# 16-bit split operands for the scores and index logits of the two A mixers

## What is computed

```python
q  = _rope(q.reshape(B, T, N_HEADS, HEAD_DIM), pos)      # 8 heads of 64
k  = _rope(k.reshape(B, T, N_HEADS, HEAD_DIM), pos)
qi = _rope(qi.reshape(B, T, IDX_HEADS, IDX_DIM), pos)    # 8 index heads of 64
ki = _rope(ki[:, :, None, :], pos)[:, :, 0, :]           # one index key
logits = jnp.einsum('bqhd,bsd->bqhs', qib, k_idx)
score = jnp.einsum('bqhs,bqh->bqs', jax.nn.relu(logits), wb) * idx_scale
score = jnp.where(causal[None], score, -jnp.inf)
_, sel = lax.top_k(score, topk)                          # 64 keys of each query
s = jnp.einsum('bqhd,bqkhd->bhqk', qb, k_sel) * att_scale
p = jax.nn.softmax(jnp.where(valid[:, None], s, -jnp.inf), axis=-1)
out = jnp.einsum('bhqk,bqkhd->bqhd', p, v_sel)
```

## Time and profile before

| | us |
|---|---|
| median of 3 runs | 1520.39 (1520.13 to 1520.46) |
| the profiled execution, its own time | 1520.18 |
| its span in the trace | 1518.1 |
| PE busy | 1510.1 (99%) |
| DVE busy | 637.6 (42%) |
| ACT busy | 475.0 (31%) |
| POOL busy | 1027.0 (68%) |
| mean granted clock of PE | 0.999 of full |

### The profile page before, as it was taken

How to read it: one execution, slowest core, us unless ns; L and a number is a source line. 1 busy time by engine, 2 the same in 40 slices (tenths; PEclk the granted TensorE clock), 3 DMA queues, 4 the chain that set the end, 5 groups by cost and what they waited for, 6 DMA issues and landing times.

```text
span 1518.1 us, 32667 instructions
## 1 busy us (share of the span) xinstructions
PE 1510.1 (99%) x13880; PEld 1174.1 (77%) x13882; DVE 637.6 (42%) x1509; ACT 475.0 (31%) x1243; POOL 1027.0 (68%) x565
## 2 busy tenths in 40 slices
PE   9999999999999999999999999999999999999998
PEld 7666888898666866669889966669888889888885
DVE  4332385445332333315844533325454535464532
ACT  3221163413221132204541232213443313343322
POOL 6976667667767677775586677773858565648653
PEclk9999999999999999999999999999999999999999
DMA  9665554455655565555545465664455554546551
GB/s 390 224 212 200 183 189 173 167 179 217 210 200 198 192 237 207 194 202 196 175 167 186 176 236 194 204 211 156 161 198 193 183 195 155 177 150 239 170 192 56
DMA packets 42625, 293.96 MB, mean 194 GB/s; under 512 B 4720, under 2 KB 5232, under 8 KB 8688
## 3 DMA queue, kind: packets, MB, share of 16 engines
q1 hardware_dynamic: 41760, 290.83, 54.5%
q10 hardware_dynamic: 720, 1.04, 0.2%
HBM read 290.81 MB, written 1.05 MB: 192 GB/s over the span
## 4 chain that ended last, share of the span: by engine, by line
PE 97%; DVE 2%; ACT 1%; issue 0%; DVEq 0%
PE ps L774 26%; PE ps L656 15%; PE ps L657 15%; PE ps L658 15%; PE ps L775 13%; PE ps L675 1%; PE ps L677 1%; PE ps L676 1%; PE ps L869 1%; PE ps L889 1%; ACT ps L1308 1%; PE ps L823 0%; PE ps L734 0%; PE ps L824 0%; PE ps L825 0%; PE ps L851 0%
## 5 line engine op out<-in xcount | busy, mean ns | idle before, releaser
L626 POOL TENSOR_TENSOR w_low<-ring 128x1024 f16<-128x1024 f32 (+1 forms) x544 | 1008.2, 1880 | 379.0 <-DMA ring<-in_w 378.7
L656 PE MATMUL ps<-hP,ring 128*128 128x256 f16 (+1 forms) x1936 | 469.1, 257 | 0.8 <-DVE work L1957 0.4
L657 PE MATMUL ps<-hP,ring 128*128 128x256 f16 (+1 forms) x1936 | 468.9, 257 | 0.0
L658 PE MATMUL ps<-hP,w_low 128*128 128x256 f16 (+1 forms) x1936 | 468.8, 257 | 0.0
L774 PE MATMUL ps<-hP,ring 128*128 128x512 f16 x1280 | 416.3, 380 | 0.0
L775 PE MATMUL ps<-hP,w_low 128*128 128x256 f16 x1280 | 349.2, 273 | 0.0
L774 PEld LDWEIGHTS ps<-hP,ring 128*128 128x128 bf16 x1280 | 125.0, 98 | 151.5 <-issue 0.4
L656 PEld LDWEIGHTS ps<-hP,ring 128*128 128x128 bf16 x1936 | 189.9, 98 | 23.3 <-issue 5.4
L657 PEld LDWEIGHTS ps<-hP,ring 128*128 128x128 bf16 x1936 | 189.2, 98 | 15.6
L658 PEld LDWEIGHTS ps<-hP,w_low 128*128 128x128 f16 x1936 | 189.2, 98 | 15.5
L774 PE MATMUL ps<-work,ring 128*128 128x512 f16 x528 | 171.8, 380 | 0.0
(11 more groups left out here) (277 smaller groups left out, 1740.8 us busy)
## 6 DMA issues: line engine op xcount, KB each, us to landing
ring<-in_w SPq DMA_DIRECT2D x261, 1024.0 KB, 4.8
ring<-in_w SPq DMA_DIRECT2D x12, 512.0 KB, 3.6
con<-in_const SPq DMA_DIRECT2D x1, 2812.0 KB, 18.3
gm<-in_gm SPq DMA_DIRECT2D x2, 1024.0 KB, 17.8
ring<-in_w SPq DMA_DIRECT2D x2, 768.0 KB, 4.9
ring<-in_w SPq DMA_DIRECT2D x2, 560.0 KB, 5.4
ring<-in_w SPq DMA_DIRECT2D x2, 544.0 KB, 3.5
xT<-in_x SPq DMA_DIRECT2D x3, 256.0 KB, 4.1
```

Of the source, the lines that this page charges most:

```text
L626: nc.gpsimd.tensor_tensor(w_low[:, c % SLOTS, a:b], ring[:, c % SLOTS, a:b], w_high[:, c % SLOTS, a:b], ALU.subtract).then_inc(split.by((c ...
L656: nc.tensor.matmul(bank, w_high[:, slot, a:a + m], rhs(k, 0), start=(k == 0), stop=False)
L657: nc.tensor.matmul(bank, w_high[:, slot, a:a + m], rhs(k, 1), start=False, stop=False)
L658: mm = nc.tensor.matmul(bank, w_low[:, slot, a:a + m], rhs(k, 0), start=False, stop=(k == kt - 1))
```

## The change

The rotated q, k, qi and ki are kept as fp16 high and low parts in `rotP`, which lies where `rot` lay. DVE's `rope` writes its sum back to the tile's PSUM bank and signals `roped_in`. ACT's new `high` copies it to the high part (`rot_high`), and DVE's new `low` subtracts and signals `taken_dve`. There are 13 such tiles in a mixer. Logits and scores take three 16-bit passes, with two heads alternating; `scores_16` (line 855) was there before for the B mixers. In PE's order one more q tile stands ahead of the first logits, and one more tile ahead of `turn(0)` and of what follows it. The rest keeps its order. The diff, cut to its core:

```diff
+IN_PARTS_A = ('q', 'k', 'qi', 'ki')
+        rotP, _ = pairs(e, 13)
         rot, e = area(e, 13, T)
 ... PE
                     def logits(p):
                         for h in (2 * p, 2 * p + 1):
-                            b = 4 + h % 3
                             if h == 0:
                                 pe.wait_ge(*taken(s, ("ki", 0)))
                             elif h < 3:
                                 pe.wait_ge(*taken(s, ("wi", h - 1)))
                             else:
                                 pe.wait_ge(*relu_done.at((s, h - 3)))
-                            o = HD * (h % 2)
-                            qi, ki = head(rot, ROT["qi"], h), rot[o:o + HD, ROT["ki"], :]
-                            nc.tensor.matmul(ps[:, b, 0:P], qi[:, 0:P], ki[:, 0:P], start=True, stop=True)
-                            nc.tensor.matmul(ps[:, b, P:PACK], qi[:, P:T], ki, start=True, stop=True
-                                             ).then_inc(logits_ready.by((s, h)), 1)
+                        for t, (a, b) in enumerate(HALVES):
+                            for i, (c, d) in enumerate(((0, 0), (0, 1), (1, 0))):
+                                for h in (2 * p, 2 * p + 1):
+                                    o = HD * (h % 2)
+                                    mm = nc.tensor.matmul(ps[:, 4 + h % 3, a:b], head(rotP, ROT["qi"], h)[:, c, span(t)],
+                                                          rotP[o:o + HD, ROT["ki"], d, 0:b - a], start=(i == 0), stop=(i == 2))
+                                    if t == 1 and i == 2:
+                                        mm.then_inc(logits_ready.by((s, h)), 1)
                     def unit(u):
-                        scores(s, u, lambda h: head(rot, ROT["q"], 4 * u + h), lambda h: head(rot, ROT["k"], 4 * u + h))
+                        first, second = slice(0, P), slice(P, T)
+                        scores_16(lambda h: head(rotP, ROT["q"], 4 * u + h), lambda h: head(rotP, ROT["k"], 4 * u + h),
+                                  ((first, first, first), (slice(P, PACK), second, slice(0, T)))
+                                  ).then_inc(scores_ready.by((s, u)), 1)
-                    gemm("q", 0), gemm("q", 1)
-                    for p, (kind, n) in enumerate((("q", 2), ("q", 3), ("k", 0), ("k", 1))):
+                    gemm("q", 0), gemm("q", 1), gemm("q", 2)
+                    for p, (kind, n) in enumerate((("q", 3), ("k", 0), ("k", 1), ("k", 2))):
                         logits(p)
                         gemm(kind, n)
-                    gemm("k", 2), gemm("k", 3)
+                    gemm("k", 3)
                     unit(0)
-                    gemm("v", 3), gemm("u", 0), gemm("u", 1), gemm("u", 2), gemm("u", 3), gemm("va", 0)
+                    gemm("v", 3), gemm("u", 0), gemm("u", 1), gemm("u", 2), gemm("u", 3), gemm("va", 0), gemm("va", 1)
                     turn(s, 0)
 ... ACT
+                    def high(kind, n):
+                        act.wait_ge(*roped_in.at((s, kind, n)))
+                        nc.scalar.activation(rotP[:, ROT[kind] + n, 0, :], ps[:, BANK_A[kind, n], 0:T], ACT.Copy
+                                             ).then_inc(rot_high.by((s, kind, n)), 1)
-                    for n in range(4):
-                        swap("qi", n)
+                    swap("qi", 0)
+                    for n in range(3):
+                        swap("qi", n + 1)
+                        high("qi", n)
                     swap("ki", 0)
+                    high("qi", 3)
                     take("wi", 0), take("wi", 1)
-                    swap("q", 0), swap("q", 1)
-                    for p, (kind, n) in enumerate((("q", 2), ("q", 3), ("k", 0), ("k", 1))):
+                    high("ki", 0)
+                    swap("q", 0), swap("q", 1), swap("q", 2)
+                    for p, (kind, n) in enumerate((("q", 3), ("k", 0), ("k", 1), ("k", 2))):
                         rectify(2 * p), rectify(2 * p + 1)
+                        high("q", p)
                         swap(kind, n)
 ... DVE
                     def rope(kind, n):
-                        nc.vector.tensor_tensor(rot[:, ROT[kind] + n, :], ps[:, b, T:2 * T], rope_a[:, r, :], ALU.add
+                        if kind in IN_PARTS_A:
+                            nc.vector.tensor_tensor(ps[:, b, 0:T], ps[:, b, T:2 * T], rope_a[:, r, :], ALU.add
+                                                    ).then_inc(roped_in.by((s, kind, n)), 1)
+                    def low(kind, n):
+                        parts = rotP[:, ROT[kind] + n, :, :]
+                        dve.wait_ge(*rot_high.at((s, kind, n)))
+                        nc.vector.tensor_tensor(parts[:, 1, :], ps[:, BANK_A[kind, n], 0:T], parts[:, 0, :], ALU.subtract
+                                                ).then_inc(taken_dve.by((s, kind, n)), 1)
-                    for n in range(4):
-                        rope("qi", n)
+                    rope("qi", 0)
+                    for n in range(3):
+                        rope("qi", n + 1)
+                        low("qi", n)
                     rope("ki", 0)
+                    low("qi", 3), low("ki", 0)
                     rope("q", 0)
                     for p in range(4):
                         head_score(2 * p), head_score(2 * p + 1)
-                        rope(*ROPED_A[6 + p])
-                    top_rounds(2, first=True)
+                        if p < 3:
+                            rope("q", p + 1)
+                        low("q", p)
+                    rope("k", 0)
+                    top_rounds(1, first=True)
                     rope("k", 1)
-                    top_rounds(1)
+                    low("k", 0)
                     rope("k", 2)
+                    low("k", 1)
                     top_rounds(1)
                     rope("k", 3)
-                    top_rounds(4)
+                    low("k", 2), low("k", 3)
+                    top_rounds(6)
```

More of the change, by code:

```diff
@@ L470, in build @@
         cos_done = signal("cos_done", [(s,) + r for s in mixers for r in roped[s]])
+        roped_in = signal("roped_in", [(s,) + r for s in MIX_A for r in ROPED_A if r[0] in IN_PARTS_A])
+        rot_high = signal("rot_high", [(s,) + r for s in MIX_A for r in ROPED_A if r[0] in IN_PARTS_A])
         swapped = signal("swapped", [(s,) + r for s in mixers for r in roped[s]])
@@ L939, in mixer_a @@
                     unit(0)
-                    gemm("v", 3), gemm("u", 0), gemm("u", 1), gemm("u", 2), gemm("u", 3), gemm("va", 0)
+                    gemm("v", 3), gemm("u", 0), gemm("u", 1), gemm("u", 2), gemm("u", 3), gemm("va", 0), gemm("va", 1)
                     turn(s, 0)
-                    gemm("va", 1), gemm("va", 2)
+                    gemm("va", 2), gemm("va", 3)
                     values(0)
-                    gemm("va", 3)
+                    gemm("ga", 0)
                     pe.wait_ge(*y_low.at((s, 0)))
                     unit(1)
-                    for n in range(5):
+                    for n in range(1, 6):
                         gemm("ga", n)
                     turn(s, 1)
-                    gemm("ga", 5), gemm("ga", 6)
+                    gemm("ga", 6), gemm("ga", 7)
                     values(1)
-                    gemm("ga", 7), gemm("gb", 0), gemm("gb", 1)
+                    gemm("gb", 0), gemm("gb", 1), gemm("gb", 2)
                     pe.wait_ge(*y_low.at((s, 1)))
@@ L960, in mixer_a @@
                         mm.then_inc(tokens_mixed.by((s, g)), 1)
-                    for n in range(2, 8):
+                    for n in range(3, 8):
                         gemm("gb", n)
@@ L1363, in mixer_a @@
                     act.wait_ge(*halved.at("bias"))
-                    for n in range(4):
-                        swap("qi", n)
+                    swap("qi", 0)
+                    for n in range(3):
+                        swap("qi", n + 1)
+                        high("qi", n)
                     swap("ki", 0)
+                    high("qi", 3)
                     take("wi", 0), take("wi", 1)
-                    swap("q", 0), swap("q", 1)
-                    for p, (kind, n) in enumerate((("q", 2), ("q", 3), ("k", 0), ("k", 1))):
+                    high("ki", 0)
+                    swap("q", 0), swap("q", 1), swap("q", 2)
+                    for p, (kind, n) in enumerate((("q", 3), ("k", 0), ("k", 1), ("k", 2))):
                         rectify(2 * p), rectify(2 * p + 1)
+                        high("q", p)
                         swap(kind, n)
-                    swap("k", 2), swap("k", 3)
-                    for n in range(4):
+                    high("k", 0)
+                    swap("k", 3)
+                    high("k", 1), high("k", 2)
+                    take("v", 0)
+                    high("k", 3)
+                    for n in range(1, 4):
                         take("v", n)
@@ L1377, in mixer_a @@
                         take("u", n)
-                    take("va", 0)
```

(11 more changed lines are left out.)

3 lines of the change are left out of this document (2 added, 1 removed).

## The result

The changed kernel takes 1537.7 us (median of 4 runs, 1537.0 to 1538.5) against 1520.35 for the kernel before. The ratio is 1.0115, 95% interval 1.0103 to 1.0126: 17.4 us slower, where 10 were forecast and the range ended at 1535.0. The direction was right; the size was not. The profiled execution took 1538.5 us, its span was 1536.6.

A forecast was written before the change was run, and what follows sets the result against it. PE, busy 99% of the span, was taken to bound the kernel. Waits of 7.6 us in A0 and 6.7 in A1, 14.3 together, less 4.1 saved, gave 10.1 us slower: 1530.4 us, range 1524.5 to 1535.

The forecast's parts named there:

- PE's saving: Logits and unit passes on PE in the A mixers: 2.06 us saved per mixer, 4.1 us in both.
- q tile 0: PE ahead of q tile 0 in each A mixer: waits 0.6 us for the `low` of qi tile 0.
- k tile 2: PE ahead of k tile 2 in each A mixer: waits 1.3 us for q 2 to be taken.
- v tile 0: PE ahead of v tile 0 in each A mixer: waits 1.0 us for the `low` of k 0.
- k tile 0: PE ahead of k tile 0: waits 4.0 us in A0 and 3.1 in A1 for q 0, with `head_score(0)` held by POOL.
- POOL's chunks land as before: POOL's run beside `head_score(0)`: borders unmoved, at 211.17 and 213.06 in A0, 210.29 and 212.17 in A1 on A0's axis.
- va tile 0: PE ahead of va tile 0 in each A mixer: waits 0.7 us for u 0's copy on ACT.
- the clock falls: Rival, behind PE's long wait: clock halves, at most 2.6 us to return; 1533 with one fall, 1535.6 with two; chance 0.12.
- the prediction's own sign of being wrong: PE behind the long wait: matmuls at twice 0.109 us apart would show the forecast wrong.
- Behind that nothing: A mixers after va tile 0: no further PE waits; the other four meetings keep 1.1 us or more.
- DVE isn't held by POOL: Rival at `head_score(0)`: POOL idle, two instructions take 0.65 us, k 0 wait 1.3 per mixer, 1525.9 us; chance 0.08.
- only the passes count: Rival at k tile 0: waits are hidden, leaving only the 4.1 us saving, 1516.3 us; chance 0.05.

The follow-up runs named there:

- e1: The changed kernel with 60 useless matmuls of 128 columns filling PE's stop ahead of k tile 0 in each A mixer; 1533.26 us.
- e2: The changed kernel with ACT copying the causal mask into PSUM ahead of time, so `head_score(0)` has one input in SBUF; 1529.21 us.
- e3: The changed kernel with q and k tiles against logits in the order of before on PE and ACT, 16-bit parts and later turn kept; 1524.42 us.
- e4: The kernel before with only the change's new orders on PE and ACT, fp32 passes and no 16-bit parts; 1523.42 us.
- e8: The 16-bit parts alone, with all orders as in the kernel before the change; 1524.47 us.
- e7: The changed kernel, PE's order untouched: mask in PSUM, u tiles 0 and 1 taken early, DVE and ACT laid out anew; 1517.01 us.
- e5: The kernel of e3 with ACT taking u tiles 0 and 1 ahead of the first unit's exponentials; 1521.28 us.
- e9: The kernel of e7 with the causal mask read from SBUF again instead of PSUM; 1522.84 us, 11 runs from 1519.4 to 1524.9.
- e6: The kernel of e2 with ACT taking u tiles 0 and 1 ahead of the first unit's exponentials; 1527.87 us.

## Why the prediction was wrong

*PE's saving* was right in kind. The start-to-start distance around a `logits` is 0.81 us (1.07 before), around a `unit` 1.31 (1.72). The heads overlap, and the pair costs 0.70 net where 0.65 was taken. 3.7 us instead of 4.1.

*The five stops* are where the prediction put them, ended by the instructions that it named. Those ahead of q tile 0, k tile 2 and v tile 0, and the one ahead of k tile 0 in A0, came within 0.5 us of their forecasts each. That of k tile 0 in A0 did so partly by luck. `head_score(0)` started at 210.25, not at 209.71: a swap behind a `high` starts 0.41 after it, where 0.28 was taken, and four of them lie ahead.

```profile
197.97 0.38 ACT L1363 ACTIVATE work<-ps 128x256 f16<-128x256 f32 x1
198.38 1.44 ACT L1339 ACTIVATE ps<-ps 32x256 f32<-32x256 f32 x4
```

Both starts lie between the same two borders of POOL, so the end stayed the same. Two stops were off by more. *k tile 0 in A1*: 4.19 instead of 3.1. The prediction took POOL's borders there from the trace before; in the changed kernel POOL's run is another one:

```profile
729.85 7.68 POOL L630 TENSOR_TENSOR w_low<-ring 128x1024 f16<-128x1024 f32 x4 [0.16 <-DMA ring<-in_w]
```

```profile
732.52 3.27 DVE L1847 SCALAR_TENSOR_TENSOR ps<-work,con 128x128 f32<-128x128 f32 x2 [2.14 <-ACT work L1370]
```

Its borders are at 731.8, 733.7 and 735.6, and the pair of instructions ended behind the last. On A0's axis (PE starts A1's q tile 0 at 721.93, 522.27 behind A0's) the last two are 211.4 and 213.3, about where A0 has them, and not 210.29 and 212.17. So the claim that POOL's chunks land as before held for A0 only. What moved them against PE in A1, no run isolates. *va tile 0*: 1.46 instead of 0.7 in both. The prediction moved the chain behind `keyset` as a block and left out that `keyset` itself has two inputs in SBUF and can be held: in A0 of the change it took 1.35 us, where it took 0.56 before, and those 0.79 us are the miss.

```profile
245.98 1.35 DVE L1903 SCALAR_TENSOR_TENSOR work<-work,con 128x384 f32<-128x384 f32 x1
```

```profile
245.03 1.89 POOL L622 TENSOR_TENSOR work<-work 128x1024 f16<-128x1024 f32 x1 [25.50 <-ACT work L1348]
246.88 15.17 POOL L630 TENSOR_TENSOR w_low<-ring 128x1024 f16<-128x1024 f32 x8
```

POOL's first row is v's low part, which it starts when v's last tile is taken, so at a fixed distance behind PE's tiles. `keyset` ended at 247.33, 0.45 behind the border to the next row. It ended 0.45 or 0.46 behind this border in both mixers of e1, e2, e3, e4 and e8 too, so the stop ahead of va tile 0 is the same 1.46 us in all of them, although DVE reached `keyset` at different times.

The Trainium skill, "SBUF — State Buffer", section "Who interferes with whom", has the rule for this: a VectorE instruction with two SBUF inputs and a GpSimd instruction that reads SBUF exclude each other. The trace agrees in all of these rows, and e2 shows the other side: the same work with one input in PSUM took 1.40 us for two heads beside the same POOL run.

*The step that failed* is the rival "the clock falls", which was given 0.12 and left out of the sum. It happened in both mixers, and the prediction's own sign of being wrong, matmuls at twice 0.109 us apart behind the long wait, is what the trace shows. The prediction itself forecast a stop of 4 us and had only stops of 1.1 us to compare with; the absence of a row was counted as evidence against, though it was none. Its price was bounded at 2.6 us a fall, and was 2.8 and 2.7. Even with two falls the prediction's figure, 1535.6, is 2.1 short of the measured median; that part is the terms above. Over both mixers the misses add up: the clock 5.5, va tile 0 1.5, k tile 0 1.0, v tile 0 0.5 and the smaller saving 0.4, less 1.1 for q tile 0 and k tile 2, make 7.9 of the 8.2 between the forecast for the profiled execution (1530.3) and its time (1538.5).

*Behind that nothing* held: no stop at a turn, at `values`, or at the end of the A mixers in the waits of the change. The rival "DVE isn't held by POOL" is what e2 forced, and gave 1529 instead of 1525.9, since the stop ahead of k tile 0 was 1.7 and 2.0 rather than 1.3 and the va stop 1.46 rather than 0.7. The rival "only the passes count" came true in e7, but needed another order on two engines.

So of the 17.4 us, with medians against the change's: filling the stop gives back 4.4 (e1); the clock and POOL's hold together are 8.5 (e2); the place of the third query tile, with what hangs on it, 13.3 (e3, not to be added to these); the late u takes about 3 (e5). What lies between e5 and e7, 4.3 us, is the mask and the order of DVE and ACT (and of the q and k tiles).

## What to carry to other kernels

A saving on the bounding engine arrives only if the engines around it still meet every due time: here 3.7 us of saved matmul time brought 16 us of stops and 5.5 of a lower clock, while the same saving with the `high` and `low` steps laid out by due time was kept. Price a stop of TensorE as the stop plus what the clock loses behind it, and when a forecast stop is longer than any in the trace, don't put the clock at nothing: here both stops of 4 us and three of six of 1.6 to 2 us were followed by a fall. Look for elementwise instructions with both inputs in SBUF beside a long GpSimd run: moving one input to PSUM took 2.3 us out of a chain at the cost of one idle-time copy.

## What was not expected of the hardware

- A TensorE stop of 1.96 us was followed by a granted clock of 0.50 in e9, in both mixers, for 3 to 4 us, and one of 1.97 in A1 of e6, while stops of 1.60 us by the rows (A0 of e2 and e6) and 1.95 us (A1 of e2) ahead of k tile 0 were not. A1 of e2, the stop and a window behind it:

```profile
730.79 0.28 PE L661 MATMUL ps<-hP,ring 128*128 128x256 f16 x1 [1.95 <-DVE work L1841]
```

```profile
732.00:734.00 2.00, 2.00 (x27) 1.00 0.16 66
```

  e2 and e6 are the same up to this place but for A0's two takes, so a stop of nearly the same length can go either way. The runs of e9 lie 5.5 us apart.
- The lower clock began while TensorE still stood (0.64 over 214 to 216 in A0 of the change, where the matmuls start at 215.50) and outlasted it by more than 5 us of dense matmuls. In e9 and in A1 of e6 it began only about half a microsecond after the matmuls had started again (in e6 they start at 729.33, and the window from 728 to 730 has a mean of 0.95).
- 60 useless matmuls of 128 columns, 59 ns each, made the kernel 4.4 us faster.
